# Expert outputs: twelve 32-partition bias sums and one store of whole rows, in place of one sum and four stores

## The reference, cut to what matters

```
def expert_ffn(xb, w_gu, b_gu, w_dn, b_dn):
    gu = xb @ w_gu + b_gu                              # 1024 -> 2 x 1024
    gate = jnp.minimum(gu[..., :D_FF], SWIGLU_LIMIT)
    up = jnp.clip(gu[..., D_FF:], -SWIGLU_LIMIT, SWIGLU_LIMIT)
    glu = gate * jax.nn.sigmoid(gate * SWIGLU_ALPHA)
    return ((up + 1) * glu) @ w_dn + b_dn              # 1024 -> 1024
```

## Time and profile before

| | |
|---|---|
| runs | 1818.70, 1816.83, 1818.67 us (median 1818.67) |
| profiled execution | 1816.69 us |
| its span | 1814.9 us, 38263 instructions |
| PE busy | 1570.0 us (87%) |
| DVE busy | 618.6 us (34%), 1247 instructions |
| ACT busy | 268.5 us (15%) |
| POOL busy | 155.6 us (9%) |
| mean granted TensorE clock | 0.895 of 2.4 GHz |

### The profile page before, as it was taken

One profiled execution on the slowest core, in us unless ns is written; L12 is line 12 of the kernel. 1 busy time (PEld: TensorE's weight loads), 2 busy tenths in 40 slices (PEclk: granted clock), 3 DMA queues, 4 the chain that ended last, 5 costly groups with the idle time before them and its releaser, 6 DMA issues.

```text
span 1814.9 us, 38263 instructions
## 1 busy us (share of the span) xinstructions
PE 1570.0 (87%) x16465; PEld 759.5 (42%) x16465; DVE 618.6 (34%) x1247; ACT 268.5 (15%) x548; POOL 155.6 (9%) x241
## 2 busy tenths in 40 slices
PE   3998888789992299999999999999999999998820
PEld 2664754555652034443443434434434344343310
DVE  1369996433346021121211212212112122121138
ACT  2231116333321000000000000000000000000001
POOL 1024104000111300000000000000000000000031
PEclk7799998655995599999999999999999999999865
DMA  9225549000443799999999999999999999985673
GB/s 347 76 104 189 186 157 346 17 4 3 161 170 115 254 364 402 404 394 407 410 396 409 397 407 409 395 409 409 397 408 394 407 409 396 407 311 214 278 250 109
DMA packets 118001, 531.91 MB, mean 293 GB/s; under 512 B 14338, under 2 KB 32296, under 8 KB 67160
## 3 DMA queue, kind: packets, MB, share of 16 engines
q1 hardware_dynamic: 85556, 471.23, 65.7%
q0 software_dynamic: 12272, 41.26, 7.0%
q10 hardware_dynamic: 20020, 17.10, 2.9%
HBM read 500.18 MB, written 29.37 MB: 292 GB/s over the span
## 4 chain that ended last, share of the span: by engine, by line
PE 74%; DVE 15%; ACT 3%; issue 3%; DMA 3%; POOL 1%; ACTq 1%; SPq 0%; DVEq 0%; POOLq 0%
PE psum L1686 38%; PE psum L1701 19%; DVE raw_ring L906 4%; DVE work L904 4%; PE psum L1649 3%; PE psum L1615 2%; PE psum L1630 2%; PE psum L1677 2%; PE psum L1670 2%; DVE final_work L1273 1%; PE psum L1623 1%; PE psum L1511 1%; POOL slot_dram L1416 1%; DMA raw_ring<-in_b_mod 1%; DMA final_work<-in_g_final 1%
## 5 line engine op out<-in xcount | busy, mean ns | idle before, releaser
L1686 PE MATMUL psum<-weight_ring,expert_work 128*32 128x512 f32 x3888 | 426.5, 593 | 1.8 <-ACT expert_work L817 1.8
L1701 PE MATMUL psum<-weight_ring,expert_work 128*32 128x256 f32 x6336 | 351.2, 381 | 3.5 <-ACT expert_work L821 3.5
L1686 PE MATMUL psum<-raw_ring,expert_work 128*32 128x512 f32 x2448 | 272.2, 598 | 11.8 <-DMA raw_ring<-in_w_gate_up 10.9
L1210 DVE TENSOR_TENSOR expert_work<-psum,expert_work 128x768 f32<-128x768 f32 x33 | 31.6, 957 | 703.5 <-PE psum L1686 703.5
L1701 PEld LDWEIGHTS psum<-weight_ring,expert_work 128*32 128x32 f32 x6336 | 203.2, 110 | 139.4 <-issue 6.4
L1686 PEld LDWEIGHTS psum<-weight_ring,expert_work 128*32 128x32 f32 x3888 | 125.2, 110 | 277.6 <-issue 271.1
L1686 PEld LDWEIGHTS psum<-raw_ring,expert_work 128*32 128x32 f32 x2448 | 77.7, 111 | 183.6 <-issue 166.5
L821 ACT ACTIVATE expert_work<-psum 128x768 f32<-128x768 f32 x33 | 26.7, 810 | 658.4 <-PE psum L1677 646.2
L1511 PE MATMUL psum<-front_ring,work 128*128 128x512 f32 (+2 forms) x320 | 117.5, 528 | 0.0
L1225 DVE TENSOR_TENSOR expert_work<-psum,expert_work 128x768 f32<-128x768 f32 x33 | 31.6, 957 | 192.7 <-PE psum L1701 192.7
L1429 POOL COPY keep<-keep 96x1 int32 (+1 forms) x34 | 6.1, 178 | 982.8 <-PE psum L1670 981.1
(11 more groups left out here) (303 smaller groups left out, 1285.2 us busy)
## 6 DMA issues: line engine op xcount, KB each, us to landing
weight_ring<-in_w_gate_up SPq DMA_DIRECT2D x162, 1024.0 KB, 16.4
weight_ring<-in_w_down SPq DMA_DIRECT2D x132, 1024.0 KB, 16.7
raw_ring<-in_w_gate_up SPq DMA_DIRECT2D x102, 1024.0 KB, 14.8
front_ring<-in_w_mod SPq DMA_DIRECT2D x12, 2048.0 KB
ys_dram<-expert_work ACTq DMA_DIRECT2D x132, 96.0 KB, 8.9
ys_dram<-raw_ring POOLq DMA_DIRECT2D x1, 8448.0 KB, 46.3
front_ring<-in_w_in SPq DMA_DIRECT2D x4, 2048.0 KB
front_ring<-in_w_mod_final SPq DMA_DIRECT2D x4, 2048.0 KB
```

Of the source, the lines that this page charges most:

```text
L1210: local(v.tensor_tensor(eg, gu_ps[:, :, 0:FF4], bg, ALU.add), 0, i)
L1686: last = mm(gu_ps[32 * q:32 * q + 32, b, :].rearrange("p (g n) -> p g n", g=2), lhsT=xT[:, k, 32 * b:32 * b + 32], rhs=w[:, q], start=(k = ...
L1701: last = mm(dn_ps[32 * q:32 * q + 32, b, :], lhsT=x, rhs=w[:, h, q], start=(s_ == 0 and h == 0), stop=(s_ == DNS - 1 and h == 1))
```

## The change

`ysb` becomes a tile of 1024 columns, of which 96 partitions are used: token slot 32b + t has its whole row on partition 32b + t. `finish` writes it by twelve sums, one for each token group and quarter, each of 32 partitions by 256: it reads PSUM on partitions 32q to 32q + 31, bank `b`, and the bias on the same partitions, and writes partitions 32b to 32b + 31, columns 256q to 256q + 255. Only the last of the twelve counts `ys_ready`. `store` becomes one transfer of 96 rows of 4 KB, and the waits on `ys_stored` count 16 for a block where they counted 64. The expert stage's work area grows by 256 words a partition. Nothing else differs.

```
--- before.py
+++ after.py
@@ -170,7 +170,7 @@
             ring = front.enter_context(nc.sbuf_tensor("front_ring", [P, FRONT_RING * SLOT], F32))
             work_t = front.enter_context(nc.sbuf_tensor("work", [P, WORK], F32))
         with ExitStack() as experts:
-            RING_WORDS, EX_WORDS = 14 * WS, D + 10 * KD * CAP
+            RING_WORDS, EX_WORDS = 14 * WS, 2 * D + 9 * KD * CAP
             assert RING_WORDS + EX_WORDS <= AREA
             ring_t = experts.enter_context(nc.sbuf_tensor("weight_ring", [P, RING_WORDS], F32))
             ex_t = experts.enter_context(nc.sbuf_tensor("expert_work", [P, EX_WORDS], F32))
@@ -317,7 +317,7 @@
         eg, eu, es = (ex.take(TB * FF4).rearrange("p (b n) -> p b n", b=TB) for _ in range(3))
         act = ex.take(TB * FF4)
         actT = ex.take(TB * FF4)
-        ysb = ex.take(TB * FF4)
+        ysb = ex.take(D)
         bias_gu = ex.take(2 * FF4)
         bias_dn = ex.take(FF4)
         bias_all = ex.take(3 * FF4)
@@ -826,9 +826,7 @@
 
             def store(i):
                 act_e.wait_ge(ys_ready, i + 1)
-                for q in range(4):
-                    dst = ys_dram[bass.ds(i * CAP, CAP), q * FF4:(q + 1) * FF4].rearrange("(b t) n -> t b n", b=TB)
-                    act_e.dma_start(dst, ysb[32 * q:32 * q + 32, :].rearrange("p (b n) -> p b n", b=TB)).then_inc(ys_stored, 16)
+                act_e.dma_start(ys_dram[bass.ds(i * CAP, CAP), :], ysb[0:CAP, :]).then_inc(ys_stored, 16)
 
             def expert_act(i):
                 take_act(i - 1)
@@ -850,7 +848,7 @@
             take_act(n_over + NE - 1)
             store(n_over + NE - 1)
 
-            act_e.wait_ge(ys_stored, (n_over + NE) * 64)
+            act_e.wait_ge(ys_stored, (n_over + NE) * 16)
             act_e.wait_ge(gathered, (n_over + NE + 1) * 16)
             act_e.wait_ge(xT_ready, n_over + NE + 1)
             note(act_e, experts_done)
@@ -1221,9 +1219,12 @@
                 dve.wait_ge(dn_read, (i + 1) * DNS)
                 dve.wait_ge(dn_spread, i + 1)
                 if not (isinstance(i, int) and i == 0):
-                    dve.wait_ge(ys_stored, i * 64)
-                v.tensor_tensor(ysb.rearrange("p (b n) -> p b n", b=TB), dn_ps, bias_dn.unsqueeze(1).to_broadcast([P, TB, FF4]),
-                                ALU.add).then_inc(ys_ready, 1)
+                    dve.wait_ge(ys_stored, i * 16)
+                for b in range(TB):
+                    for q in range(4):
+                        ps = slice(32 * q, 32 * q + 32)
+                        ins = v.tensor_tensor(ysb[32 * b:32 * b + 32, q * FF4:(q + 1) * FF4], dn_ps[ps, b, :], bias_dn[ps, :], ALU.add)
+                ins.then_inc(ys_ready, 1)
 
             def spread_gu(src, row):
                 v.stream_shuffle(bias_gu, src[:, 0:2 * FF4], [row] * 32).then_inc(gu_spread, 1)
```

## The result

The changed kernel takes 1827.93 us (median of 6 runs, 1824.89 to 1832.17) against 1819.56 us for the kernel before (6 runs, 1816.83 to 1821.77): a ratio of 1.0048, with a 95% interval of 1.0036 to 1.0061. It is slower by 8.4 us by the medians; 8.7 were forecast, and a time of 1826.4 us.

A forecast was written before the change was run, and what follows sets the result against it. PE was taken to bound the expert stage, with a chain of waits deciding the last 145 us. Terms 2.6 + 2.75 + 3.35 = 8.7 us on a base of 1817.7 gave 1826.4 us; range 1822 to 1830.5.

The forecast's parts named there:

- The bound: Mid expert stage: PE alone sets the 32.96 us period; sums and store fit beside it, costing nothing.
- Twelve sums of 0.43: VectorE's bias sums: twelve without overlap, 0.43 us start to start, 5.15 us against 0.96, last result 4.19 us later.
- Place 1: Overflow block's weight loads, waiting for the shuffle behind block 30's sums: PE restarts 1.6 to 3.55 us later, taken as 2.6.
- Place 2: ScalarE's copy behind expert 31's store, before PE's last down projection: both move 2.75 us later (4.19 - 1.44).
- Place 3: After PE's end, last sum and store landing release the final stage: 3.35 us later (4.19 - 0.84).
- The sum: Whole kernel: the three places at the end add 2.6 + 2.75 + 3.35 = 8.7 us.
- The base of 1817.7 us: Starting time of the kernel before, taken halfway between about 1816.8 and 1818.7 us, to which 8.7 was added.
- Overlap: Rival: VectorE's sums overlap, pitch 0.34 us, 3.20 us later each time; 5.7 us slower, 1823.4 us; chance 0.12.
- Dearer sums: Rival: VectorE's sums cost more than 0.43, at 0.48 us each; 10.5 us slower, 1828.2 us; chance 0.08.
- cheap sums: Rival: at the three ends, sums at 0.21 us each nearly paid for by spared issues; 1.6 us slower, 1819.3; chance 0.04.
- a shifted steady stage: Rival: sums and store over 10 us hold ACT's copy, 31 periods by 1 us, 31 us slower, 1849; chance 0.02.

The follow-up runs named there:

- the doubled sums: Changed kernel with each of the twelve sums of blocks 0 to 29 done once more into a spare tile; 1827.70 us, 1.0041 to the kernel before.
- the run with the quadrant kept: Kernel before with twelve sums in the old layout, quarter as outer loop, and the four old stores; 1828.77 us, 1.0050 to the kernel before.
- old ends: Changed kernel with the old sum and old four stores for blocks 31 and 32 alone; 1820.78 us, 1.0003 to the kernel before.
- copy first: Changed kernel with each store moved behind ScalarE's copy of the next block's turned activations; 1826.94 us, 1.0039 to the kernel before.

## Why the prediction was right, and where its terms were off

*The bound.* PE sets the stage's pace and DVE has room: confirmed by the period of 32.96 in every kernel and by the doubled sums. From the second half of gate/up of block 1 to block 30's projection, with the sums of 30 blocks between, it is 1000.04 to 1000.05 us in all eleven profiles.

*Twelve sums of 0.43.* 5.15 us predicted, 5.19 measured (1675.04 to 1680.23). L1124 was the right row, and the run with the quadrant kept shows why the pair L1211 and L1212 was not.

*Place 1.* SP was to go on 3.55 us later; from the projection's end to the first load it is 7.67 us where it was 4.09, 3.58 more. The landing was put at 4.8 to 6.75 us, 5.8 in the middle, and took 5.31. So it is 2.13 us on the gap in place of 2.6. The clock's 0.49 behind it makes the place cost 2.62, which is luck: in the kernels with the same waits at this place (old ends, copy first, sums doubled) this half takes 13.15, 11.86 and 11.83 us.

*Place 2.* 2.75 predicted, 2.72 measured. That "the clock gives nothing back and takes little" was not borne out: the last projection was 1.10 us shorter. That is not the change's doing either. Over all profiles with a gap of 4 us and more it takes either 11.9 to 12.3 or 13.0 to 13.3 us, with no order by the gap's length (after 7.13 us: 11.95, 13.33 and 13.24; after 4.4: 11.88 and 13.05).

*Place 3.* This term was mis-sized: 3.35 predicted, 3.89 measured. The step that failed is the line drawn between the final stage's stores, 2.5 us for 384 KB; the store took 3.00, and 2.97 to 2.99 in the four other kernels that have it at the end. Why 96 rows take longer than those 128 rows of the same length at 2.8 stays open; no run varied it. The page that the prediction set beside it ("DMA: Bandwidth & Descriptors" of the Trainium skill, "Anatomy of one DMA") gives 2.9, an estimate for another kind of queue, and is nearer.

*The sum.* 8.7 predicted; 8.25 behind the drift in the profiles; 8.4 by the medians. That it is so close is partly luck. The three gaps add up to 8.74 since 0.47 too much at place 1 meets 0.54 too little at place 3, and the clock, which the sum left out, put 0.49 on one place and took 1.10 off the other. The base of 1817.7 us was 1.9 below the six runs' median, so 1826.4 is 1.5 too low.

*The rivals.* Overlap: refuted for this order, shown for the other. Dearer sums, cheap sums, a shifted steady stage: none. (The cheap rival's +0.5 at place 1 would be 0.1 by the way used for the overlap rival; it changes no chance.)

## What to carry to other kernels

Added work on an engine that was busy 34% of the time was free in 30 of 33 blocks and cost 8 us in the last three: read the end of a pipelined loop as a stage of its own, since waits that the next block's work covers elsewhere lie bare there. Before trading instructions for transfers, look at who waits for the last instruction and who for the transfer. And it may be worth more to move the waiting instruction than to shorten what it waits for: here moving two of them gave 18 us.

## What the runs showed of the hardware beyond that

A VectorE sum of 32x256 from PSUM starts 0.33 us after the one before it when both read and write the same quadrants, and 0.43 when they change, for 0.42 us of its own. Reading another quadrant is enough: in the changed kernel nine of a dozen's sums write the partitions that the sum before them wrote, and they too start 0.43 us apart.

On TensorE's clock the profiles give no length of gap that is safe. A gap of 1.99 us, 1.07 of them idle, left the granted clock at 1.00; each gap of 4.4 us and more was followed by slower matmuls, and what the last projection lost (1.3 to 2.8 us against 10.57) did not follow the length of the gap. But at the start of the expert stage, behind an idle time of 1.84 to 1.85 us that all eleven profiles show, the clock fell to 0.50 in the changed kernel's profile (half of gate/up in 12.13 us) and in none of the other ten (10.51).

And the eleven profiles, with the same period throughout, start block 30's projection anywhere between 1653.9 and 1664.4 us: a single profile pair cannot tell 8 us, and only its parts can.
